# A convolution's last block: its gates moved ahead, twelve of its taps on TensorE, and the order of GpSimd and ScalarE around it

## The chip, the core and the metric

The kernel runs on one core of one Trainium2 chip. The metric is the device time of one execution in microseconds (us); the median of several runs is given. The core has TensorE (matrix products, PE in the profile; PEld is its weight load), VectorE (DVE), ScalarE (ACT), GpSimd (POOL) and SyncE (SP), which issues most transfers. The engines run their own instruction streams and meet through semaphores.

## What is computed

A trunk of two layers over 512 tokens of width 1024, in float32. The first layer mixes tokens by a Conformer convolution, the second by attention; each is followed by a squared-ReLU MLP. Only the convolution matters here:

```python
def conformer_conv(h, pw1_w, pw1_b, dw_w, dw_b, ln_g, ln_b, pw2_w, pw2_b):
    a = h @ pw1_w + pw1_b
    u, gate = jnp.split(a, 2, axis=-1)
    u = u * jax.nn.sigmoid(gate)
    y = depthwise_causal_conv(u, dw_w, width=31) + dw_b
    y = layernorm(y, ln_g, ln_b)
    y = jax.nn.silu(y)
    return y @ pw2_w + pw2_b
```

## The kernel before

Channels lie on the 128 partitions, tokens (512) along the free axis, so the 1024 channels are 8 blocks of 128, numbered j = 0 to 7. A float32 product is made of three matmuls of a high and a low part (hi x hi, lo x hi, hi x lo), and each operand is split into such parts by ScalarE (high) and GpSimd or VectorE (low).

For each block, the first pointwise product gives u and its gate in two PSUM banks. `gates` (VectorE, two instructions) scales both into `tmp`; `sigmoid` (ScalarE) and `gated` (VectorE) put u into `upad`, with 31 columns of padding. The 31 taps of the depthwise convolution are then shared out:

- TensorE takes `PE_TAPS` = 7 of them: a tap is a product with a diagonal matrix, three matmuls for its parts (lines 793 to 795, function `conv`). It needs `uhi` (ScalarE, `u_hi`), `ulo` (GpSimd, `u_lo`) and the block's diagonals `diaghi`, `diaglo`, which ScalarE builds from the identity, 14 small instructions of 128x128 (`diagonals`, line 1205).
- ScalarE makes the first two taps into two PSUM banks (`first_taps`, lines 1274 and 1276; they wait for semaphore `acc`, the join of the block in front) and `POOL_TAPS` = 5 products in SBUF (`pool_taps`, line 1284), which GpSimd adds into `y` in four sums (`tap_sums`, line 500).
- VectorE takes the other 17, one instruction each, in two chains that go on from ScalarE's first two (`tap`, line 1729). `join` adds the two chains into `acc1`, `finish` adds TensorE's bank to it.
- GpSimd's `y_total` adds `acc1` to `y` of that block, and `y` to `sumsq`, the sum over blocks from which the mean is made.

The last block, j = 7, has `MORE_TAPS` = 4 x `LOOP_TAPS` = 8 of VectorE's taps moved to TensorE. Their diagonals (`morehi`, `morelo`) are built ahead by ScalarE, `LOOP_TAPS` taps (4 small instructions) in each of the four blocks of its loop (blocks 2 to 5, `more_diagonals`, line 1197). `conv(KB - 1, 1, MORE_TAPS)` runs these taps first and waits for the block's ordinary diagonals only behind them.

The order on each engine is the order of the code. VectorE runs all 17 taps of block 6 and puts the gates of block 7 behind tap 14 and `gated` behind tap 16 (`last_gates`), then joins block 6, finishes it, and does the 9 taps left of block 7. Once `y` of block 7 is complete on VectorE (line 1807), TensorE sums all blocks into the mean, as a product of `ones` with `sumsq` (line 836) and with `y` of block 7 (line 839), with small products in between whose results nobody reads (`keep_warm`). VectorE subtracts the mean (line 1811), ScalarE squares, TensorE sums the squares by columns, ScalarE takes the root, VectorE the reciprocal, TensorE spreads it, and the normalised blocks go through silu into the second pointwise product (`N_PW2`). Its weights lie in units 0 to 3, split high by ScalarE (`split_hi`) and low by GpSimd (`conv_lo`), units 0 and 1 in block 6 and units 2 and 3 at the end. SyncE refills a pair of units once both low parts are made.

Of the kernel before, what the change touches and what calls it, by code (L numbers as in the profile page):

```python
# [13 lines left out]
KB = D // P  # L14
# [14 lines left out]
LOOP_TAPS = 2  # L29
# [121 lines left out]
def build(nc, x, g_mix_pre, g_mix_post, g_ffn_pre, g_ffn_post, conv_pw1_w, conv_pw1_b, conv_dw_w,  # L151
# [194 lines left out]
    with nc.Block() as block:  # L346
# [105 lines left out]
        def _(pool):  # L452
# [41 lines left out]
            def tap_sums(j):  # L494

                for k in range(1, POOL_TAPS):
                    pool.wait_ge(s["tap_act"], ACT_TAPS * j + (3 + k))
                    if k > 1:
                        pool.wait_ge(s["y_sum"], y_sums(j) + (k - 1))
                    g.tensor_tensor(blk(y, j), blk(y, j), prods[:, k - 1, :], ALU.add).then_inc(s["y_sum"], 1)  # L500
# [7 lines left out]
            def y_total(j, r):  # L508

                at_ = y_sums(j + 1) + POOL_SUMS  # L510
                pool.wait_ge(s["y_done"], j + 1)
                pool.wait_ge(s["y_sum"], at_)
                g.tensor_tensor(blk(y, j), blk(y, j), acc1[:, r, :], ALU.add).then_inc(s["y_sum"], 1)
                pool.wait_ge(s["y_sum"], at_ + 1)
                g.tensor_tensor(sumsq[:, :], sumsq[:, :], blk(y, j), ALU.add).then_inc(s["y_sum"], 1)
# [34 lines left out]
            for u in (0, 1):  # L550
                conv_lo(N_PW2, u)
            tap_sums(KB - 2)
            u_lo(KB - 1, 1)
            y_total(KB - 3, 1)
            tap_sums(KB - 1)
            y_total(KB - 2, 0)
            for u in (2, 3):
                conv_lo(N_PW2, u)
# [49 lines left out]
        def _(pe):  # L608
# [226 lines left out]
            pe.wait_ge(s["y_sum"], y_sums(KB))  # L835
            pe.matmul(psum[:, STAT, :], ones[:, :], sumsq[:, :], start=True, stop=False)
            keep_warm(WARM_TAPS)
# [281 lines left out]
        def _(act):  # L1119
# [159 lines left out]
            def pool_taps(j, r):  # L1279

                for k in range(POOL_TAPS):
# [11 lines left out]
            def conv_step(n, more=None, rs=range(2)):  # L1293
                for r in rs:
# [13 lines left out]
            conv_step(3, None, range(1))  # L1308
            sigmoid(KB - 1)
            u_hi(KB - 1, 1)  # L1310
            first_taps(KB - 1, 1)
            pool_taps(KB - 1, 1)
            for u in (2, 3):
                split_hi(N_PW2, u)
# [324 lines left out]
        def _(dve):  # L1639
# [150 lines left out]
            def last_gates(i):  # L1790

                if i == 14:
                    gates(3, 1)
                if i == 16:
# [19 lines left out]
            d.tensor_tensor(m[:, 7, :], m[:, 6, :], m[:, 7, :], ALU.add).then_inc(s["c_pair"], 1)  # L1814
            inverse(ST_VAR)
# [560 lines left out]
```

## Time and profile before

| | us |
|---|---|
| median of 3 runs | 1178.49 (1177.1 to 1179.14) |
| the profiled execution | 1181.36 |
| its span (first to last instruction) | 1179.7 |
| TensorE busy | 1144.3 (97%) |
| VectorE busy | 907.5 (77%) |
| ScalarE busy | 660.1 (56%) |
| GpSimd busy | 191.1 (16%) |

The profile is of one execution, whose span lies 1.66 us under its own time. The convolution takes the first 178 us or so of it. Matmuls are pipelined: one of 512 columns is shown 0.39 us long, and the next starts 0.23 us after it. "Idle before" in a row is the time the engine stood, with what ended it. The granted clock (PEclk) is 1.00 at 2.4 GHz and 0.50 at 1.2 GHz.

### The profile page before, as it was taken

To read this page: it belongs to the slowest core of one execution; us is meant where nothing else is said; L and a number is where in the kernel's file an instruction comes from. 1 tells how busy PE (TensorE), PEld (TensorE's weight loads), DVE (VectorE), ACT (ScalarE), POOL (GpSimd) and SP (SyncE) were. 2 spreads that over 40 slices of the span, in tenths; PEclk is the share of its full clock that TensorE was granted. 3 is DMA by queue.
4 is the path that set the end of the run, shared out by engine and by line. 5 is a ranking of instruction groups with operands and counts; after the bars stand their busy time and mean duration, and the time that the engine had idled before them with its cause. 6 is when DMAs were issued, how large, how long until landed. Compare 5 with 4: busy or idle time off the path is not lost. (4 is left out here: it accounts for less than half of the span.)

```text
span 1179.7 us, 16069 instructions
## 1 busy us (share of the span) xinstructions
PE 1144.3 (97%) x5598; PEld 962.5 (82%) x5598; DVE 907.5 (77%) x1368; ACT 660.1 (56%) x1106; POOL 191.1 (16%) x176
## 2 busy tenths in 40 slices
PE   7999799999999999999999999999999999999996
PEld 6788688978888888887888888888888888888885
DVE  4899955689479579589888888884797588586698
ACT  4878847566354444345677666665566453443453
POOL 5588860120000000003420001000300000000000
PEclk9999989999999999999999999999999999999998
DMA  4422211520621523412222232222423414215301
GB/s 149 108 71 71 71 39 33 183 69 5 211 73 36 178 72 105 145 36 54 55 54 54 55 87 71 72 72 72 143 72 108 143 36 163 88 36 179 107 19 72
DMA packets 103676, 102.30 MB, mean 87 GB/s; under 512 B 4622, under 2 KB 86542, under 8 KB 103611
## 3 DMA queue, kind: packets, MB, share of 16 engines
q1 hardware_dynamic: 103532, 101.29, 27.0%
q8 instruction: 38, 0.62, 0.2%
q10 hardware_dynamic: 78, 0.16, 0.1%
q14 instruction: 28, 0.22, 0.1%
HBM read 99.34 MB, written 2.10 MB: 86 GB/s over the span
## 5 line engine op out<-in xcount | busy, mean ns | idle before, releaser
L617 PE MATMUL psum<-hhi,whi 128*128 128x512 f32 x792 | 312.6, 395 | 0.6 <-DVE tmp L1908 0.3
L619 PE MATMUL psum<-hhi,wlo 128*128 128x512 f32 x792 | 308.8, 390 | 0.0
L618 PE MATMUL psum<-hlo,whi 128*128 128x512 f32 x792 | 308.5, 390 | 0.0
L1149 ACT ACTIVATE whi<-mraw 128x1024 fp32r<-128x1024 f32 x176 | 185.3, 1054 | 145.1 <-PE psum L884 113.6
L1657 DVE TENSOR_TENSOR wlo<-mraw,whi 128x1024 fp32r<-128x1024 f32 x176 | 213.9, 1221 | 44.4 <-ACT whi L1149 44.4
L882 PE MATMUL psum<-whi,aop_hi 128*128 128x512 f32 x448 | 175.3, 391 | 0.8 <-DVE wlo L1657 0.8
L619 PEld LDWEIGHTS psum<-hhi,wlo 128*128 128x128 f32 x792 | 148.6, 188 | 31.8
L884 PE MATMUL psum<-whi,aop_lo 128*128 128x512 f32 x448 | 174.4, 389 | 0.0
L883 PE MATMUL psum<-wlo,aop_hi 128*128 128x512 f32 x448 | 174.3, 389 | 0.0
L617 PEld LDWEIGHTS psum<-hhi,whi 128*128 128x128 f32 x792 | 148.8, 188 | 30.9 <-issue 2.0
L618 PEld LDWEIGHTS psum<-hlo,whi 128*128 128x128 f32 x792 | 148.8, 188 | 29.1
L1388 ACT ACTIVATE pair<-tmp 128x512 f32<-128x512 f32 x64 | 40.4, 632 | 156.0 <-DVE tmp L1908 156.0
L1908 DVE SCALAR_TENSOR_TENSOR tmp<-psum,rinv 128x512 f32<-128x512 f32 x64 | 44.0, 689 | 78.9 <-PE psum L619 76.3
L882 PEld LDWEIGHTS psum<-whi,aop_hi 128*128 128x128 f32 x448 | 84.1, 188 | 18.2 <-DVE wlo L1657 1.2
L884 PEld LDWEIGHTS psum<-whi,aop_lo 128*128 128x128 f32 x448 | 84.1, 188 | 17.7
L883 PEld LDWEIGHTS psum<-wlo,aop_hi 128*128 128x128 f32 x448 | 84.1, 188 | 17.1
L1729 DVE SCALAR_TENSOR_TENSOR psum<-upad,vec,psum 128x512 f32<-128x512 f32 x120 | 80.5, 752 | 3.6 <-ACT psum L1274 3.6
L1962 DVE TENSOR_TENSOR mraw<-mraw 128x1024 f32<-128x1024 f32 x64 | 78.0, 1221 | 1.7
L1127 ACT ACTIVATE whi<-wraw 128x1024 fp32r<-128x1024 f32 x51 | 52.7, 1050 | 7.8 <-PE psum L619 4.7
L574 POOL CAST wfhi<-wfraw 128x128 fp32r<-128x128 f32 x8 | 5.0, 629 | 302.0 <-DVE wlo L1657 302.0
L624 PE MATMUL psum<-hhi,whi 128*128 128x256 f32 (+1 forms) x128 | 41.6, 325 | 3.5 <-DVE hlo L1663 3.3
L1646 DVE TENSOR_TENSOR wlo<-wraw,whi 128x1024 fp32r<-128x1024 f32 x35 | 42.8, 1225 | 2.6 <-ACT whi L1127 2.6
(253 smaller groups left out, 1946.9 us busy)
## 6 DMA issues: line engine op xcount, KB each, us to landing
mraw<-in_mlp_w_up SPq DMA_DIRECT2D x64, 512.0 KB, 5.3
mraw<-in_mlp_w_down SPq DMA_DIRECT2D x64, 512.0 KB, 4.6
wraw<-in_conv_pw_w SPq DMA_DIRECT2D x20, 512.0 KB, 4.5
wraw<-in_attn_w_in SPq DMA_DIRECT2D x16, 512.0 KB, 4.6
wraw<-in_attn_w_in SPq DMA_DIRECT2D x16, 256.0 KB, 3.1
wraw<-in_attn_w_o SPq DMA_DIRECT2D x8, 512.0 KB, 4.0
xin<-in_x SPq DMA_DIRECT2D x4, 512.0 KB, 6.8
wraw<-in_conv_pw_w SPq DMA_DIRECT2D x8, 256.0 KB, 6.7
```

What stands on the lines that cost most here:

```text
L617: pe.matmul(o, whi[:, u, kb, :], xhi, start=start, stop=False)
L618: pe.matmul(o, whi[:, u, kb, :], xlo, start=False, stop=False)
L619: return pe.matmul(o, wlo[:, u, kb, :], xhi, start=False, stop=stop)
L882: pe.matmul(o, ah, wh, start=kt == 0 and (not kept or c == 0), stop=False)
L883: pe.matmul(o, ah, wl, start=False, stop=False)
L884: return pe.matmul(o, al, wh, start=False, stop=kt == 3 and (not kept or c == CHUNKS - 1))
L1127: a.activation(whi[:, u, :, :], wraw[:, r, :, c * P:(c + 1) * P], ACT.Copy).then_inc(w_hi[r], 2 if single else 1)
L1149: a.activation(split_unit(whi, e), raw_unit(c, e_), ACT.Copy).then_inc(s["m_hi"], 1)
L1657: d.tensor_tensor(split_unit(wlo, e), raw_unit(c, e_), split_unit(whi, e).bitcast(F32), ALU.subtract).then_inc(s["m_ready"], 1)
L1729: d.scalar_tensor_tensor(dst, upad[:, r, t:t + S], vcol(V_DW + t, j), src, ALU.mult, ALU.add).then_inc(s["tap"], 1)
L1908: d.scalar_tensor_tensor(tmp[:, 2 + j % 2, :], psum[:, j % 4, :], 0.0, rinv[:, :], ALU.max, ALU.mult).then_inc(s["up_relu"], 1)
L1962: d.tensor_tensor(to, to, mraw[:, p[PLUS[i]], half], ALU.add).then_inc(s["t_sum"], 1)
```

## The change

- `LOOP_TAPS` is 3, so `MORE_TAPS` is 12: TensorE runs 12 extra taps of block 7, VectorE 5, and ScalarE builds six, not four, extra small diagonals in each of the four looped blocks.
- VectorE does the gates of block 7 behind tap 4 of block 6 and `gated` behind tap 5.
- ScalarE: in block 6 three pool taps come first, then block 7's `sigmoid` and `u_hi`, then the other two; `first_taps` of block 7, its diagonals, its pool taps, and all four splits of `N_PW2` behind.
- GpSimd: in block 6 two sums, `u_lo` of block 7, two sums, then `y_total` of block 5. Behind the sums of block 7 `y_total` of block 6 leaves out the addition into `sumsq`. Only units 0 and 1 of `N_PW2` are split there, behind that total.
- TensorE adds one product of `ones` with `y` of block 6 to the mean. It waits for one count less on `y_sum`.
- VectorE makes the low parts of units 2 and 3 of `N_PW2`, ahead of the reciprocal of the variance.

```diff
-LOOP_TAPS = 2
+LOOP_TAPS = 3
...
-            def y_total(j, r):
+            def y_total(j, r, add=True):
...
                 g.tensor_tensor(blk(y, j), blk(y, j), acc1[:, r, :], ALU.add).then_inc(s["y_sum"], 1)
+                if not add:
+                    return
...
             u_lo(KB - 2, 0)
-            for u in (0, 1):
-                conv_lo(N_PW2, u)
-            tap_sums(KB - 2)
+            tap_sums(KB - 2, range(1, 3))
             u_lo(KB - 1, 1)
+            tap_sums(KB - 2, range(3, POOL_TAPS))
             y_total(KB - 3, 1)
             tap_sums(KB - 1)
-            y_total(KB - 2, 0)
-            for u in (2, 3):
+            y_total(KB - 2, 0, add=False)
+            for u in (0, 1):
                 conv_lo(N_PW2, u)
...
-            pe.wait_ge(s["y_sum"], y_sums(KB))
+            pe.wait_ge(s["y_sum"], y_sums(KB) - 1)
             pe.matmul(psum[:, STAT, :], ones[:, :], sumsq[:, :], start=True, stop=False)
+            pe.matmul(psum[:, STAT, :], ones[:, :], y[:, KB - 2, :], start=False, stop=False)
...
-            conv_step(3, None, range(1))
+            sigmoid(KB - 2)
+            first_taps(KB - 2, 0)
+            u_hi(KB - 2, 0)
+            pool_taps(KB - 2, 0, range(3))
             sigmoid(KB - 1)
             u_hi(KB - 1, 1)
+            pool_taps(KB - 2, 0, range(3, POOL_TAPS))
             first_taps(KB - 1, 1)
+            next_diagonals(KB - 2, 0)
             pool_taps(KB - 1, 1)
-            for u in (2, 3):
+            for u in range(4):
                 split_hi(N_PW2, u)
...
-                if i == 14:
+                if i == 4:
                     gates(3, 1)
-                if i == 16:
+                if i == 5:
                     gated(KB - 1, 1)
...
             d.tensor_tensor(m[:, 7, :], m[:, 6, :], m[:, 7, :], ALU.add).then_inc(s["c_pair"], 1)
+            for u in (2, 3):
+                split_lo(N_PW2, u)
             inverse(ST_VAR)
```

On ScalarE, from the splits in block 6 to the products of block 7. Before (of the 14 diagonals the first two stand):

```order
L1127 ACTIVATE whi<-wraw 128x1024 [waits unit0,raw0] x2
L1284 ACTIVATE y<-upad,vec 128x512
L1284 ACTIVATE prods<-upad,vec 128x512 [waits y_sum] x4
L1205 ACTIVATE diaghi<-ident,dwhi 128x128 [waits conv_done]
L1205 ACTIVATE diaglo<-ident,dwlo 128x128
L1259 ACTIVATE tmp<-tmp,vec 128x512 [waits glu_g]
L1266 ACTIVATE uhi<-upad 128x544 [waits conv_done,glu_u]
L1274 ACTIVATE psum<-upad,vec 128x512 [waits acc,glu_u]
L1276 ACTIVATE psum<-upad,vec 128x512
L1284 ACTIVATE y<-upad,vec 128x512
L1284 ACTIVATE prods<-upad,vec 128x512 [waits y_sum] x4
```

In the changed kernel, from the `uhi` of block 6, with the first two diagonals:

```order
L1268 ACTIVATE uhi<-upad 128x544 [waits conv_done,glu_u]
L1286 ACTIVATE y<-upad,vec 128x512
L1286 ACTIVATE prods<-upad,vec 128x512 [waits y_sum] x2
L1261 ACTIVATE tmp<-tmp,vec 128x512 [waits glu_g]
L1268 ACTIVATE uhi<-upad 128x544 [waits conv_done,glu_u]
L1286 ACTIVATE prods<-upad,vec 128x512 [waits y_sum] x2
L1276 ACTIVATE psum<-upad,vec 128x512 [waits acc,glu_u]
L1278 ACTIVATE psum<-upad,vec 128x512
L1207 ACTIVATE diaghi<-ident,dwhi 128x128 [waits conv_done]
L1207 ACTIVATE diaglo<-ident,dwlo 128x128
L1286 ACTIVATE y<-upad,vec 128x512
L1286 ACTIVATE prods<-upad,vec 128x512 [waits y_sum] x4
```

The sigmoid and `uhi` of block 7 have moved up into block 6's products, and the diagonals from ahead of that sigmoid to behind the two instructions that wait for `acc`.

On GpSimd, from `ulo` of block 6 to the end of the taps. Before:

```order
L491 TENSOR_TENSOR ulo<-upad,uhi 128x544 [waits u_hi]
L505 TENSOR_TENSOR wlo<-wraw,whi 128x1024 [waits w_hi0] x2
L500 TENSOR_TENSOR y<-y,prods 128x512 [waits tap_act]
L500 TENSOR_TENSOR y<-y,prods 128x512 [waits y_sum,tap_act] x3
L491 TENSOR_TENSOR ulo<-upad,uhi 128x544 [waits u_hi]
L513 TENSOR_TENSOR y<-y,acc_73 128x512 [waits y_sum,y_done]
L515 TENSOR_TENSOR sumsq<-sumsq,y 128x512 [waits y_sum]
L500 TENSOR_TENSOR y<-y,prods 128x512 [waits tap_act]
L500 TENSOR_TENSOR y<-y,prods 128x512 [waits y_sum,tap_act] x3
L513 TENSOR_TENSOR y<-y,acc_73 128x512 [waits y_sum,y_done]
L515 TENSOR_TENSOR sumsq<-sumsq,y 128x512 [waits y_sum]
```

In the changed kernel:

```order
L491 TENSOR_TENSOR ulo<-upad,uhi 128x544 [waits u_hi]
L500 TENSOR_TENSOR y<-y,prods 128x512 [waits tap_act]
L500 TENSOR_TENSOR y<-y,prods 128x512 [waits y_sum,tap_act]
L491 TENSOR_TENSOR ulo<-upad,uhi 128x544 [waits u_hi]
L500 TENSOR_TENSOR y<-y,prods 128x512 [waits y_sum,tap_act] x2
L513 TENSOR_TENSOR y<-y,acc_73 128x512 [waits y_sum,y_done]
L517 TENSOR_TENSOR sumsq<-sumsq,y 128x512 [waits y_sum]
L500 TENSOR_TENSOR y<-y,prods 128x512 [waits tap_act]
L500 TENSOR_TENSOR y<-y,prods 128x512 [waits y_sum,tap_act] x3
L513 TENSOR_TENSOR y<-y,acc_73 128x512 [waits y_sum,y_done]
```

The two splits into `wlo` ahead of block 6's sums are gone; `ulo` of block 7 stands between these sums; the last addition into `sumsq` is gone.

On VectorE, from the taps of block 6 to its join. Before:

```order
L1729 SCALAR_TENSOR_TENSOR psum<-upad,vec,psum 128x512 [waits tap_act] x2
L1729 SCALAR_TENSOR_TENSOR psum<-upad,vec,psum 128x512 [waits tap] x13
L1740 TENSOR_TENSOR tmp<-psum,rinv 128x512 [waits glu_u,unit1]
L1742 TENSOR_TENSOR tmp<-psum,rinv 128x512
L1729 SCALAR_TENSOR_TENSOR acc_73<-upad,vec,psum 128x512 [waits y_sum,tap]
L1729 SCALAR_TENSOR_TENSOR psum<-upad,vec,psum 128x512 [waits tap]
L1754 SCALAR_TENSOR_TENSOR upad<-tmp,vec 128x512 [waits u_ready,tap_act,glu_s,glu_t]
L1760 TENSOR_TENSOR acc_73<-psum,acc_73 128x512 [waits tap]
```

In the changed kernel:

```order
L1736 SCALAR_TENSOR_TENSOR psum<-upad,vec,psum 128x512 [waits tap_act] x2
L1736 SCALAR_TENSOR_TENSOR psum<-upad,vec,psum 128x512 [waits tap] x3
L1747 TENSOR_TENSOR tmp<-psum,rinv 128x512 [waits glu_u,unit1]
L1749 TENSOR_TENSOR tmp<-psum,rinv 128x512
L1736 SCALAR_TENSOR_TENSOR psum<-upad,vec,psum 128x512 [waits tap]
L1761 SCALAR_TENSOR_TENSOR upad<-tmp,vec 128x512 [waits u_ready,tap_act,glu_s,glu_t]
L1736 SCALAR_TENSOR_TENSOR psum<-upad,vec,psum 128x512 [waits tap] x9
L1736 SCALAR_TENSOR_TENSOR acc_73<-upad,vec,psum 128x512 [waits y_sum,tap]
L1736 SCALAR_TENSOR_TENSOR psum<-upad,vec,psum 128x512 [waits tap]
L1767 TENSOR_TENSOR acc_73<-psum,acc_73 128x512 [waits tap]
```

The two gates and the writing of `upad` for block 7 have moved up by ten and eleven taps.

## Rows read from the trace of the kernel before

**Rows 1.** Window: busy us (instructions) PE, PEld, DVE, ACT, POOL; PEclk, DMA share, GB/s.

```profile
104.00:120.00 16.00, 16.00 (x72) 13.14 (x71) 15.49 (x23) 13.04 (x31) 14.26 (x10) 1.00 0.20 66
```

**Rows 2.** Timeline of VectorE, blocks 6 and 7: start, us, operation, [idle before].

```profile
130.07 1.78 DVE L1754 SCALAR_TENSOR_TENSOR upad<-tmp,vec 128x512 f32<-128x512 f32 x1
...
132.71 9.97 DVE L1729 SCALAR_TENSOR_TENSOR psum<-upad,vec,psum 128x512 f32<-128x512 f32 x15 [0.26 <-ACT psum L1274]
142.59 0.69 DVE L1740 TENSOR_TENSOR tmp<-psum,rinv 128x512 f32<-128x512 f32 x1
...
145.10 0.98 DVE L1754 SCALAR_TENSOR_TENSOR upad<-tmp,vec 128x512 f32<-128x512 f32 x1
146.00 0.68 DVE L1760 TENSOR_TENSOR acc<-psum,acc 128x512 f32<-128x512 f32 x1
...
156.44 0.69 DVE L1804 TENSOR_TENSOR acc<-acc,y 128x512 f32<-128x512 f32 x1 [2.10 <-POOL y L500]
160.61 0.69 DVE L1807 TENSOR_TENSOR y<-psum,acc 128x512 f32<-128x512 f32 x1 [3.48 <-PE psum L795]
163.15 4.88 DVE L1811 SCALAR_TENSOR_TENSOR y<-psum,y 128x512 f32<-128x512 f32 x8 [1.85 <-PE psum L839]
...
172.05 0.18 DVE L1679 RECIPROCAL irms<-rms 128x4 f32<-128x4 f32 x1 [2.49 <-ACT rms L1180]
```

**Rows 3.** Timeline of TensorE, blocks 6 and 7 and the statistics.

```profile
136.16 0.39 PE L793 MATMUL psum<-uhi,diaghi 128*128 128x512 f32 x1
...
148.24 0.80 PE L793 MATMUL psum<-uhi,morehi 128*128 128x512 f32 x1 [7.02 <-POOL ulo L491]
...
155.44 0.39 PE L793 MATMUL psum<-uhi,diaghi 128*128 128x512 f32 x1
...
160.34 1.02 PE L836 MATMUL psum<-sumsq,ones 128*128 128x512 f32 x2
161.20 1.05 PE L635 MATMUL psum<-ones 128*128 128x128 f32 x8
```

**Rows 4.** Timeline of ScalarE, blocks 6 and 7.

```profile
129.00 0.72 ACT L1259 ACTIVATE tmp<-tmp,vec 128x512 f32<-128x512 f32 x1 [0.63 <-DVE tmp L1740]
...
138.74 0.39 ACT L1205 ACTIVATE diaghi<-ident,dwhi 128x128 fp32r<-128x128 f32 x1
...
142.54 0.39 ACT L1205 ACTIVATE diaglo<-ident,dwlo 128x128 fp32r<-128x128 f32 x1
...
146.78 0.78 ACT L1274 ACTIVATE psum<-upad,vec 128x512 f32<-128x512 f32 x1
...
148.11 0.71 ACT L1284 ACTIVATE y<-upad,vec 128x512 f32<-128x512 f32 x1
148.72 2.55 ACT L1284 ACTIVATE prods<-upad,vec 128x512 f32<-128x512 f32 x4
```

**Rows 5.** Timeline of GpSimd, blocks 5 to 7.

```profile
130.02 1.29 POOL L513 TENSOR_TENSOR y<-y,acc 128x512 f32<-128x512 f32 x1
...
133.94 1.37 POOL L491 TENSOR_TENSOR ulo<-upad,uhi 128x544 fp32r<-128x544 f32 x1 [0.94 <-ACT uhi L1266]
...
150.74 5.60 POOL L500 TENSOR_TENSOR y<-y,prods 128x512 f32<-128x512 f32 x4
156.47 1.80 POOL L513 TENSOR_TENSOR y<-y,acc 128x512 f32<-128x512 f32 x1
```

**Rows 6.** Page, part 5: a split of 128x1024 on VectorE.

```profile
L1657 DVE TENSOR_TENSOR wlo<-mraw,whi 128x1024 fp32r<-128x1024 f32 x176 | 213.9, 1221 | 44.4 <-ACT whi L1149 44.4
```

**Rows 7.** Timeline of TensorE in a later stage.

```profile
584.67 0.39 PE L975 MATMUL psum<-hhi,wfhi 128*128 128x256 f32 x1 [1.51 <-DVE hlo L2131]
```

**Rows 8.** Windows of that stage, TensorE: busy us (instructions), PEclk, DMA share, GB/s.

```profile
585.00:585.50 0.50, 0.50 (x5) 0.55 0.00 0
...
591.50:592.00 0.50, 0.50 (x5) 0.62 0.00 0
```

**Rows 9.** Window of rows 1's kind, in the convolution's norm.

```profile
172.00:173.00 1.00, 1.00 (x7) 1.00 (x6) 0.18 (x1) 0.98 (x2) 0.00 (x0) 0.52 0.00 0
```

More of the change, by code:

```diff
@@ L492, in u_lo, with tap_sums @@
                                 ALU.subtract).then_inc(s["u_ready"], 1)
-            def tap_sums(j):
-                for k in range(1, POOL_TAPS):
+            def tap_sums(j, ks=range(1, POOL_TAPS)):
+                for k in ks:
                     pool.wait_ge(s["tap_act"], ACT_TAPS * j + (3 + k))
@@ L1277, in first_taps, with pool_taps @@
                              scale=vcol(V_DW + 1, j)).then_inc(s["tap_act"], 1)
-            def pool_taps(j, r):
-                for k in range(POOL_TAPS):
+            def pool_taps(j, r, ks=range(POOL_TAPS)):
+                for k in ks:
                     if k > 0 and not (isinstance(j, int) and j == 0):
@@ L1291, in next_diagonals, with conv_step @@
                 diagonals(j + 1, 1 - r)
-            def conv_step(n, more=None, rs=range(2)):
-                for r in rs:
+            def conv_step(n, more=None):
+                for r in range(2):
                     j = 2 * n + r
```

## The prediction

> **What bounds the kernel now.** I read the stage table first: in a block of the convolution's loop TensorE is busy for all 16.00 us and VectorE for 15.49 [rows 1], so neither ScalarE's nor GpSimd's work there sets the time, as long as it fits. Then the timelines of the four engines around the last two blocks (6 and 7), because the diff changes nothing else of weight. The reader is to see who is last there. VectorE finishes its taps, stands 2.10 us for GpSimd's sums and 3.48 us for TensorE, and writes y[7] at 160.61 [rows 2]. TensorE had stood 7.02 us before block 7's taps, because VectorE's gates for block 7 come behind 15 taps of block 6, and it ran the first of those taps at half rate [rows 3]. GpSimd ended its sums for block 7 at 156.34 and its total of block 6 at 158.27; the addition into sumsq behind it, of the length of the total at 130.02 (1.29), brings it to about 159.6 [rows 5], just ahead of TensorE's need at 160.34 [rows 3]. So before, TensorE is last and GpSimd is 0.7 us behind being last. Everything after hangs on the mean: VectorE's subtraction starts at 163.15 [rows 2], and all later stages follow that point one for one, since TensorE, VectorE and ScalarE work in a chain from there to the second pointwise product. I therefore work out where 163.15 goes.
>
> **The sum is made against the profiled execution** (1181.36 us, span 1179.7); the median of the three runs is 1178.49, 2.87 lower. I carry the difference over to the median unchanged.
>
> **Loop.** Each of the four looped blocks gets 2 more small diagonals on ScalarE, 2 x 0.292 us = 0.58 ([rows 4]: 13 steps of them from 138.74 to 142.54). ScalarE stands 0.63 us ahead of the sigmoid that follows [rows 4], so 0.05 is left, and VectorE waits for nothing else of ScalarE there. Cost 0; if the cover were gone it would be under 0.1 a block. The splits of the convolution weights grow by 4 columns of 8 blocks at the start: nothing that I can price above 0.05.
>
> **Gates of block 7 earlier.** Block 6's taps start at 132.71 and take 9.97 for 15, 0.665 each [rows 2]; five end at 136.0. The gates also wait for TensorE's last unit, whose last matmul lies right ahead of the first tap matmul of block 6 at 136.16 [rows 3] and so ends at about 136.3; with 0.1 us of signalling the gates start at 136.45. Before, 2.51 us lay from gates to gated (142.59 to 145.10) with two taps between [rows 2]; now there is one, so gated starts at 138.3. From gated's start to TensorE's first tap matmul it took 3.14 us (145.10 to 148.24 [rows 2, 3]), so TensorE starts block 7 at 141.45. It has just ended block 6 (21 matmuls from 136.16 at 0.233, [rows 3]: 21 from 155.44 to 160.34). The pause of 7.02 shrinks to about 0.3, and the slow start goes: before, 24 matmuls took 7.20 us against 24 x 0.233 = 5.6. That is the gain, 6.8 + 1.6 us of TensorE.
>
> **Twelve taps on TensorE.** 12 x 3 = 36 matmuls x 0.233 = 8.4: they end at 149.85. VectorE keeps 5 taps of block 7, not 9 (2.7 us less).
>
> **Where it goes wrong: the diagonals.** The seven ordinary taps of block 7 need their diagonals. Before, ScalarE built them at 138.74, ahead of block 7's sigmoid. Now they stand behind first_taps of block 7, and these wait for `acc`, the join of block 6, which VectorE reaches only behind the remaining 11 taps. gated ends and the next operation starts 0.90 later (145.10 to 146.00 [rows 2]), at 139.2; 11 x 0.665 = 7.3 gives the join at 146.5. Before, first_taps came 0.78 behind the join's start (146.00 to 146.78 [rows 2, 4]): now 147.3, against 146.78. ScalarE, which has only uhi (from gated's end) and two products of 0.61 to do, stands from about 141.2 till then. first_taps take 1.33 (146.78 to 148.11), so the diagonals run from 148.6, 14 x 0.292 = 4.1, to 152.7. TensorE stands from 150.0 to 152.9, then runs 21 x 0.233 = 4.9 to 157.9 if its clock holds.
>
> **GpSimd's sums become last.** ScalarE's products for GpSimd (the pool taps) of block 7 come behind the diagonals: the first at 152.7, the second ends 0.61 + 0.71 later, 154.05 [rows 4]. GpSimd's four sums start at 154.15; from their start to the total behind them is 5.73 (150.74 to 156.47 [rows 5]), so the total of block 6 starts at 159.9, 3.4 us later than before. It takes 1.80 where VectorE adds y and acc1 from 0.03 us ahead of it (156.44 [rows 2]), and 1.29 where it is itself 0.05 ahead (130.02, and VectorE's instruction at 130.07 then takes 1.78 [rows 2, 5]). The last sum of block 7 releases the same two again, so I take 1.80: 161.7, lower bound 161.2. The sum into sumsq is no longer waited for (GpSimd does not do it). VectorE's y[7] is written by about 161.3 and is not last.
>
> The Trainium skill (SBUF — State Buffer, section "SBUF: two separate sides") says that VectorE operations with two SBUF inputs and GpSimd operations exclude each other for a whole instruction, whichever starts first. By that rule the total is 1.80 if VectorE starts first again; both pairs of rows agree, and without the rule the sum would be 0.5 lower.
>
> **The extra matmul.** From TensorE's first statistic matmul to VectorE's subtraction it was 160.34 to 163.15 = 2.81 us. The new one on y[6] is the same form, two passes, 0.86 (160.34 to 161.20 [rows 3]). 161.75 + 2.81 + 0.86 = 165.4: **+2.3 us** against 163.15, with the clock at its upper level (2.4 GHz).
>
> **The clock.** TensorE now pauses 2.9 us (150.0 to 152.9) and 3.8 us (157.9 to 161.7), with only 4.9 us of work between. In this trace a pause of 1.51 us before 584.67 was followed by a granted clock of 0.55 in the half us from 585.0, that is, mostly the lower level of 1.2 GHz, which lasted until about 591.6; and the 7.02 us pause by the 1.6 us of loss above [rows 3, 7, 8]. The statistic matmuls (3.5 us of work) would run partly slow. Bounds: 0 and 1.6 us. Since the pause is longer than the one at 584.67, I take 1.1. Of the stretch behind it I take no change: before, the clock was already low from 172.0 [rows 9].
>
> **Two splits on VectorE.** The low parts of two weight units leave GpSimd and stand between the pair sum and the reciprocal. VectorE stands 2.49 us there [rows 2]; 2 x 1.221 = 2.44 [rows 6]. Cost 0 to 0.1. On SP's queue the refill of these units waits for these splits, and the small loads stand behind it; what they bring is used only in the second half of the second pointwise product and later: nothing. On GpSimd the other two splits come behind the total, two of them where two stood before, ahead of the squares that GpSimd adds, which move by the sum themselves. Nothing.
>
> Sum: +2.3 + 1.1 = +3.4. 1181.36 + 3.4 = 1184.8 for the profiled execution, **1178.5 + 3.4 = 1181.9 for the median**.
>
> **Rivals.** 0.2% is 2.4 us, about what a measurement of this kernel can tell from no change.
> (a) *The order costs little*: the total takes 1.29, the clock holds, and with the pauses elsewhere the half-rate stretch at 172 (granted clock 0.52 [rows 9]; it delays the broadcast, by my estimate some 0.9 us) falls away: +1.8 - 0.9 = +0.9, or +1.8 without the last: 1179.4 to 1180.3, no change. For it: a clock's fall is not seen behind every short pause. Chance 0.26.
> (b) *gated meets GpSimd.* gated took 1.78 at 130.07 while GpSimd's total ran (130.02), 0.98 at 145.10 [rows 2, 5]. GpSimd's two sums of block 6 now start behind its ulo, at 135.3 [rows 5], and end at 135.3 + 2 x 1.40 (5.60 for four) = 138.1, 0.2 ahead of gated. If they are 0.2 late, gated, the 11 taps, the join, the diagonals and the sums all come 0.8 later: +4.2, 1182.7. Chance 0.12; it decides from a sum that ends behind 138.3.
> (c) *Faster, by the clock alone.* A later stage ran at half rate from 585.0 to 591.5 [rows 8], which costs 6.5 / 2 = 3.2 us, and the stretch at 172 costs 0.9. Both hang on where pauses fall. If the shift moved the pauses so that both stayed at 2.4 GHz, and the statistics too: +1.8 - 0.9 - 3.2 = -2.3, and -2.6 if the signals come 0.3 sooner than taken: 1175.9. It decides if the granted clock in the stage behind 582 stays at 1.00. Against it: the median of the runs lies 2.87 below the profiled one, so these may not have that stretch to lose. Chance 0.07.
> (d) *The change does what it is named for* and the diagonals are not waited for: TensorE ends at 141.45 + 57 x 0.233 = 154.7, and the pool taps come right behind first_taps, at 148.6. Their second product ends at 149.9, the sums lead to the total at 150.0 + 5.73 = 155.7, it ends at 157.5, and the subtraction starts at 157.55 + 3.67 = 161.2: -1.9, 1176.6. That needs ScalarE to build the diagonals in its pause before the join, and the order of its instructions in the program says that it doesn't. Chance 0.02.
>
> **How the numbers follow.** The forecast has 0.53, (a) 0.26, (b) 0.12, (c) 0.07, (d) 0.02. Slower: forecast 0.53 + (b) 0.12 = 0.65, less 0.01 at the edge; same 0.28 with (a) and (d); faster 0.08. Range: from (a)'s middle with its clock gain, 1178.8, to (b) with the full 1.6 of clock (+2.3 + 0.8 + 1.6 = +4.7) and 1 us for later stages, 1184.2.
>
> **What would show it.** In the changed kernel: TensorE's taps of block 7 start near 141.5 with nearly no pause; 36 matmuls; then a pause of 2.9 ended by ScalarE's diagonals; first_taps of block 7 near 147.3, idle ScalarE for some 6 us before; GpSimd's first sum of block 7 near 154.2 and the total to 161.7; the first statistic matmul released by GpSimd, and VectorE's subtraction between 165.4 and 167. Wrong if the subtraction comes before 163.2, or if TensorE ends the taps after GpSimd's total.

## The result

The changed kernel ran at a median of 1184.45 us (1182.08 to 1185.74, 6 runs) against 1177.62 us (1176.76 to 1179.14, 6 runs), and the ratio of the times is 1.0044, 95% interval 1.0031 to 1.0057. It is slower. (The ratio is the one on record for the whole comparison; the two medians alone lie 6.83 us or 0.58% apart, a little outside the interval.) The same kernel, measured once more beside the kernel before in a later comparison (e9_again below), came out at 1.0016 (1.0006 to 1.0027). So the loss is there both times, and its size is not one number; what of it the runs explain is said below.

Head of the page of the profiled execution (its own time 1184.01 us): span, TensorE's busy time, and the granted clock in 40 slices.

```profile
span 1182.3 us, 16112 instructions
...
PE 1147.0 (97%) x5612; PEld 962.7 (81%) x5612; DVE 907.1 (77%) x1366; ACT 662.7 (56%) x1114; POOL 185.4 (16%) x173
...
PEclk9999999999999999999999999999999999999998
```

The timelines of the changed kernel, in which rows 2 to 5 have their counterparts. VectorE first: start, length, operation, idle before.

```profile
136.44 0.69 DVE L1747 TENSOR_TENSOR tmp<-psum,rinv 128x512 f32<-128x512 f32 x1 [0.26 <-PE psum L620]
...
138.31 0.75 DVE L1761 SCALAR_TENSOR_TENSOR upad<-tmp,vec 128x512 f32<-128x512 f32 x1
...
146.34 0.69 DVE L1767 TENSOR_TENSOR acc<-psum,acc 128x512 f32<-128x512 f32 x1
...
159.61 0.69 DVE L1811 TENSOR_TENSOR acc<-acc,y 128x512 f32<-128x512 f32 x1 [7.56 <-POOL y L500]
160.34 0.69 DVE L1814 TENSOR_TENSOR y<-psum,acc 128x512 f32<-128x512 f32 x1
166.95 4.88 DVE L1818 SCALAR_TENSOR_TENSOR y<-psum,y 128x512 f32<-128x512 f32 x8 [5.92 <-PE psum L841]
...
173.27 2.35 DVE L1653 TENSOR_TENSOR wlo<-wraw,whi 128x1024 fp32r<-128x1024 f32 x2
175.93 0.18 DVE L1686 RECIPROCAL irms<-rms 128x4 f32<-128x4 f32 x1 [0.31 <-ACT rms L1182]
```

Gates at 136.44 and gated at 138.31 are where 142.59 and 145.10 were [rows 2]. From there to the join of block 6 at 146.34 nothing waits. Behind its taps of block 7 VectorE stands 7.56 us for GpSimd, writes y of block 7 at 160.34, 0.27 earlier than before, and stands 5.92 us for TensorE: the subtraction starts at 166.95, against 163.15 [rows 2]. The two splits (2.35) fit in front of the reciprocal.

ScalarE and GpSimd:

```profile
139.65 1.32 ACT L1286 ACTIVATE prods<-upad,vec 128x512 f32<-128x512 f32 x2
147.13 0.78 ACT L1276 ACTIVATE psum<-upad,vec 128x512 f32<-128x512 f32 x1 [6.15 <-DVE acc L1767]
...
148.47 0.39 ACT L1207 ACTIVATE diaghi<-ident,dwhi 128x128 fp32r<-128x128 f32 x1
...
152.56 0.71 ACT L1286 ACTIVATE y<-upad,vec 128x512 f32<-128x512 f32 x1
```

```profile
153.96 5.56 POOL L500 TENSOR_TENSOR y<-y,prods 128x512 f32<-128x512 f32 x4 [7.28 <-ACT prods L1286]
159.66 1.77 POOL L513 TENSOR_TENSOR y<-y,acc 128x512 f32<-128x512 f32 x1
```

`first_taps` of block 7 come at 147.13 behind the join, with 6.15 us of idle time before them; before, they came at 146.78 [rows 4]. Behind them stand the 14 diagonals (148.47 to 152.5) and only then the products, at 152.56 instead of 148.11. GpSimd waits 7.28 us for the second product, starts its sums at 153.96 instead of 150.74 and the total at 159.66 instead of 156.47 [rows 5].

TensorE, and its granted clock in three windows of half a microsecond (third number from the end):

```profile
141.24 0.51 PE L794 MATMUL psum<-uhi,morehi 128*128 128x512 f32 x1
...
152.70 0.50 PE L794 MATMUL psum<-uhi,diaghi 128*128 128x512 f32 x1 [2.79 <-ACT diaglo L1207]
...
161.48 1.95 PE L837 MATMUL psum<-sumsq,ones 128*128 128x512 f32 x2 [3.63 <-POOL y L513]
163.22 1.92 PE L838 MATMUL psum<-y,ones 128*128 128x512 f32 x2
...
165.89 1.02 PE L841 MATMUL psum<-y,ones 128*128 128x512 f32 x2
```

```profile
162.00:162.50 0.50, 0.50 (x2) 0.50 0.00 0
...
165.00:165.50 0.50, 0.50 (x6) 0.94 0.00 0
...
592.50:593.00 0.50, 0.50 (x4) 0.50 0.00 0
```

It starts block 7 at 141.24, 7.0 us earlier than before, stands 2.79 us for the diagonals and 3.63 us for GpSimd's total, and runs the two first statistic products at 1.2 GHz: 1.95 and 1.92 us, against 1.02 [rows 3].

### The profile page after: what moved, and what is told of

Its sections match the earlier page's. It is cut to its first block and busy times, and to the rows that moved or that the text cites. A ratio compares the mean times of both kernels' runs of the same rounds, so it can differ in the third digit from the quotient of the medians.

```text
span 1182.3 us, 16112 instructions
## 1 busy us (share of the span) xinstructions
PE 1147.0 (97%) x5612; PEld 962.7 (81%) x5612; DVE 907.1 (77%) x1366; ACT 662.7 (56%) x1114; POOL 185.4 (16%) x173
## 5 line engine op out<-in xcount | busy, mean ns | idle before, releaser
L884 PE MATMUL psum<-whi,aop_hi 128*128 128x512 f32 x448 | 175.3, 391 | 0.8 <-DVE wlo L1664 0.8
L1736 DVE SCALAR_TENSOR_TENSOR psum<-upad,vec,psum 128x512 f32<-128x512 f32 x116 | 78.1, 752 | 3.6 <-ACT psum L1276 3.6
```

What stands on the lines that cost most here:

```text
L884: pe.matmul(o, ah, wh, start=kt == 0 and (not kept or c == 0), stop=False)
L1736: d.scalar_tensor_tensor(dst, upad[:, r, t:t + S], vcol(V_DW + t, j), src, ALU.mult, ALU.add).then_inc(s["tap"], 1)
```

## The experiments

The same point of the program lies up to a microsecond apart in the profiles (`gated` of block 6 starts between 129.38 and 130.45), so points are counted from that start (130.07 before, 130.16 in the changed kernel), where all these kernels are still alike. The fourth column is a length, the others are starts; all are in us.

| kernel | first_taps of block 7 | total of block 6 | first statistic product | from it to the subtraction | subtraction | ratio of the times (95%) |
|---|---|---|---|---|---|---|
| before | 16.71 | 26.40 | 30.27 | 2.81 | 33.08 | 1 |
| changed | 16.97 | 29.50 | 31.32 | 5.47 | 36.79 | 1.0044 (1.0031 to 1.0057) |
| e9_again | 16.99 | 29.53 | 31.36 | 3.77 | 35.13 | 1.0016 (1.0006 to 1.0027) |
| e1_diag_first | 17.00 | 25.49 | 27.32 | 5.45 | 32.77 | 0.9992 (0.9980 to 1.0003) |
| e2_warm | 16.98 | 29.53 | 34.23 | 3.67 | 37.90 | 1.0040 (1.0025 to 1.0055) |
| e10_warm16 | 16.98 | 29.52 | 31.35 | 3.78 | 35.13 | 1.0014 (1.0002 to 1.0027) |
| e3_eight_taps | 17.03 | 29.54 | 31.37 | 3.77 | 35.14 | 1.0004 (0.9991 to 1.0017) |
| e4_full_total | 16.96 | 29.50 | 32.67 | 2.92 | 35.59 | 1.0021 (1.0011 to 1.0031) |
| e5_before_twelve | 16.71 | 26.38 | 34.34 | 2.81 | 37.15 | 1.0026 (1.0015 to 1.0036) |
| e6_splits_back | 17.01 | 29.54 | 31.37 | 5.47 | 36.84 | 1.0039 (1.0022 to 1.0057) |
| e7_free | 10.71 | 22.26 | 24.47 | 3.66 | 28.13 | 0.9940 (0.9918 to 0.9961) |
| e12_free_again | 10.72 | 22.24 | 24.50 | 3.67 | 28.17 | 0.9959 (0.9945 to 0.9972) |
| e8_nowait_only | 10.71 | 23.30 | 25.14 | 3.78 | 28.92 | 0.9960 (0.9945 to 0.9975) |
| e11_free_eight | 10.73 | 22.17 | 25.92 | 3.67 | 29.59 | 0.9959 (0.9946 to 0.9973) |

**Is the chain through ScalarE the cause?** e1_diag_first moves one call of the changed kernel:

```diff
+            next_diagonals(KB - 2, 0)
             first_taps(KB - 1, 1)
-            next_diagonals(KB - 2, 0)
             pool_taps(KB - 1, 1)
```

> The changed kernel with one step moved: ScalarE builds block 7's diagonals ahead of first_taps of block 7, in its pause of 6.15 us before the join. The theory (the end of the stage is set by the chain join, first_taps, diagonals, pool taps, GpSimd's four sums, total): the products start at 148.5 instead of 152.56, the total ends 4.1 us earlier, at 157.3, TensorE has no pause between its 12 and its 7 taps and ends at 154.5, and VectorE's subtraction comes at 161.1 to 162.9 instead of 166.95: 4.1 to 5.9 us faster than the changed kernel, 0.3 to 2.1 faster than the kernel before. Rival (the extra matmuls and the pause of TensorE set the time, not GpSimd's sums): the subtraction moves by less than 2 us.

Timeline of that kernel, TensorE's first statistic product and VectorE's subtraction:

```profile
157.15 1.54 PE L837 MATMUL psum<-sumsq,ones 128*128 128x512 f32 x2 [2.63 <-POOL y L513]
...
162.60 4.87 DVE L1818 SCALAR_TENSOR_TENSOR y<-psum,y 128x512 f32<-128x512 f32 x8 [5.90 <-PE psum L841]
```

The total came 4.01 us earlier (29.50 to 25.49), as theory had it, and with it the subtraction (36.79 to 32.77). The statistics ran at 1.2 GHz again (5.45 from their start to the subtraction), so it came at the slow end of what was expected. The time falls back to that of the kernel before. TensorE has no pause before its ordinary taps here and still stands 2.63 us for GpSimd's total, so it is not TensorE's matmuls or its pause that cost the 4 us, but the 14 diagonals in front of GpSimd's products.

**And if ScalarE need not wait?** e7_free takes away the reason for the wait (block 7's first taps write banks 0 and 1, the chains that the join of block 6 ends lie in banks 6 and 7) and puts the products ahead of the diagonals:

```diff
-                if not (isinstance(j, int) and j == 0):
+                if not (isinstance(j, int) and j in (0, KB - 1)):
                     act.wait_ge(s["acc"], j)
...
             first_taps(KB - 1, 1)
-            next_diagonals(KB - 2, 0)
             pool_taps(KB - 1, 1)
+            next_diagonals(KB - 2, 0)
```

> The changed kernel, where first_taps of block 7 no longer wait for the join of block 6 (they write banks 0 and 1, which that join does not read), and the order behind them on ScalarE is pool taps, then diagonals. Theory: first_taps at 140.9, the five products end at about 144.7, diagonals at 148.7, before TensorE asks for them at 149.9; GpSimd's sums of block 7 run 146.7 to 152.3 and the total to 154.2; TensorE runs 57 matmuls without a pause to 154.5 and goes on into the statistics; the subtraction at 158.2. That is 8.7 us earlier than the changed kernel and 5.0 earlier than the kernel before: 1172.6 against a median of 1177.6. Rival (the two-SBUF-input meetings of VectorE and GpSimd and the clock eat it): 160 or later.

Timeline of e7_free over all engines, the rows that moved:

```profile
141.14 0.77 ACT L1276 ACTIVATE psum<-upad,vec 128x512 f32<-128x512 f32 x1
...
146.92 5.62 POOL L500 TENSOR_TENSOR y<-y,prods 128x512 f32<-128x512 f32 x4
...
154.90 1.02 PE L837 MATMUL psum<-sumsq,ones 128*128 128x512 f32 x2
...
158.56 4.87 DVE L1818 SCALAR_TENSOR_TENSOR y<-psum,y 128x512 f32<-128x512 f32 x8 [2.71 <-PE psum L841]
```

ScalarE goes on at 141.14 without a pause, GpSimd's sums follow its sumsq at 146.92, and TensorE comes from its last tap straight to the statistics at 154.90. The subtraction lies 28.13 behind gated, 4.95 us less than before (expected 5.0). The median was 1172.03 beside 1178.94 before (0.9940). e12_free_again is the same kernel on another chip.

> e7_free once more, for more executions: 0.994 to 0.996 of the kernel before, subtraction 28.1 behind gated of block 6. If the first result was a matter of the clock in a few executions, the ratio comes out nearer to 0.998.

28.17 and 0.9959 (1173.23 beside 1178.95): the place is the same to 0.04 us, and this version beats both kernels, each time.

e8_nowait_only takes only the wait away and keeps the order.

> The changed kernel, where only the wait of first_taps of block 7 for the join of block 6 is gone; the order on ScalarE stays first_taps, diagonals, pool taps. Counted from the start of gated of block 6 (130.16 in the changed kernel, whose subtraction comes 36.8 behind it; 33.1 in the kernel before; 28.1 in e7_free): first_taps at +10.8, diagonals to +16.2, the second product ends at +17.6, the sums at +23.3, the total at +25.1, subtraction at +28.8. So the wait is worth nearly all, and the order diagonals before products costs 0.7 against e7_free. Rival (the order matters as much as the wait): +31 or more.

ScalarE's `first_taps` and VectorE's subtraction in e8_nowait_only:

```profile
140.12 0.77 ACT L1276 ACTIVATE psum<-upad,vec 128x512 f32<-128x512 f32 x1
...
158.33 4.87 DVE L1818 SCALAR_TENSOR_TENSOR y<-psum,y 128x512 f32<-128x512 f32 x8 [3.48 <-PE psum L841]
```

The subtraction lies at 28.92, with a ratio of 0.9960: the wait is worth 6.2 us of the chain (against 35.13 in e9_again, statistics at 2.4 GHz in both), the order behind it 0.8.

**The twelve taps.** e3_eight_taps is the changed kernel with `LOOP_TAPS = 2`.

> The changed kernel with 8 instead of 12 extra taps of block 7 on TensorE, all else as changed. Theory: TensorE's 12 fewer matmuls end 2.8 us earlier, at 146.8, and only lengthen its pause before the diagonals (still at 152.65); VectorE's four more taps end at 154, ahead of GpSimd's sums at 159.5. The subtraction stays at 166.9 within 0.2, unless the longer pause lowers the clock earlier. Rival (TensorE's 36 matmuls for extra taps cost time): 2.8 us faster.

TensorE in e3_eight_taps:

```profile
151.99 0.79 PE L794 MATMUL psum<-uhi,diaghi 128*128 128x512 f32 x1 [5.58 <-ACT diaglo L1207]
...
160.77 1.12 PE L837 MATMUL psum<-sumsq,ones 128*128 128x512 f32 x2 [1.40 <-POOL y L513]
```

The statistics start at 31.37 against 31.32: in the order of the work the four taps more on TensorE move nothing. The subtraction is 1.65 earlier than in the changed kernel, though, because the clock fell at 150.1, in the longer pause of 5.58 us, and was back at 2.4 GHz at 156.9, before the statistics. In that profile this is the clock and not the taps: e9_again shows the same 3.77 with twelve. In the executions the two can't be told apart. Of e3_eight_taps ten lie between 1179.1 and 1182.4 us, eight of them within 0.7 us of each other; of the twelve-tap kernel twelve lie between 1179.2 and 1183.1 in e9_again and six between 1182.1 and 1185.7 in the first comparison. That the longer pause puts the fall of the clock under the taps every time, and that twelve taps cost time in this way, was not tested.

e5_before_twelve does the twelve taps alone, in the kernel before (`LOOP_TAPS = 3` there and nothing else).

> The kernel before with 12 instead of 8 extra taps of block 7 on TensorE and nothing else. Before, TensorE was the last to end the taps, so 12 more matmuls at 0.233 us put all behind it off by 2.8 us: subtraction at 165.9 to 166.0 against 163.15. Rival (VectorE's four taps fewer help): no later than before.

Its timeline, TensorE's first tap and first statistic product and VectorE's subtraction:

```profile
147.90 0.80 PE L793 MATMUL psum<-uhi,morehi 128*128 128x512 f32 x1 [7.01 <-POOL ulo L491]
...
164.08 1.02 PE L836 MATMUL psum<-sumsq,ones 128*128 128x512 f32 x2
...
166.89 4.88 DVE L1811 SCALAR_TENSOR_TENSOR y<-psum,y 128x512 f32<-128x512 f32 x8 [1.85 <-PE psum L839]
```

+4.07 where 2.8 was expected: 12 matmuls at 0.233 are 2.8. For the other 1.3 the clock accounts: it stayed at 1.2 GHz for 6.1 us from the first tap at 147.90 (3.2 us before), and half of the difference is 1.45 us. Where TensorE is last, as in the kernel before, the taps cost; and the ratio of 1.0026 (3.1 us) says the same.

e11_free_eight is e7_free with eight.

> e7_free with 8 instead of 12 extra taps of block 7 on TensorE. Theory: with ScalarE free, GpSimd's total ends at +24.1 behind gated of block 6 and TensorE's 57 matmuls at +24.5, so the two are level; with 45 matmuls TensorE ends at +21.7 and waits for GpSimd; VectorE's nine taps end its y[7] at about +25.8, ahead of the product that needs it (+26.8). Subtraction at +27.8, 0.3 earlier than e7_free, or the same: the twelve taps bring nothing there. Rival (the twelve taps pay once ScalarE is out of the way): 1 us or more later.

Timeline of e11_free_eight, TensorE and VectorE:

```profile
149.16 0.50 PE L794 MATMUL psum<-uhi,diaghi 128*128 128x512 f32 x1 [2.39 <-ACT diaglo L1207]
...
154.09 2.06 DVE L1811 TENSOR_TENSOR acc<-acc,y 128x512 f32<-128x512 f32 x1
...
155.72 1.02 PE L837 MATMUL psum<-sumsq,ones 128*128 128x512 f32 x2
```

1.46 later than e7_free, not 0.3 earlier. Two things were left out. The first are the diagonals: with the products ahead of them they are ready at 149.1, so TensorE, done with eight taps at about 146.8, stands 2.39 us for them; with twelve it comes to them when they are ready. The 2.8 us of taps taken off thus made only a pause: 21 matmuls at 0.233 behind 149.16 end 24.3 behind `gated`, where e7_free has its statistics at 24.47. The second is the clock, which was at 1.2 GHz from 150.6 to 154.0, under these 21 matmuls; half of that, 1.7 us, is by my estimate what put the statistics at 25.92. VectorE, with four more taps, also met GpSimd's split in its addition (2.06 us instead of 0.69). The time is nevertheless that of e7_free on the same chip (0.9959 both), so between 8 and 12 taps nothing is decided by time.

**The clock.** e2_warm and e10_warm16 fill TensorE's pause before the statistics with small products whose results nobody reads, 30 of them in e2_warm (shown), 16 in e10_warm16:

```diff
+            keep_warm(30, 2)
             pe.wait_ge(s["y_sum"], y_sums(KB) - 1)
```

> The changed kernel with 30 small matmuls of TensorE, whose results nobody reads, in its pause of 3.63 us between block 7's last tap and the first statistic matmul, so that it doesn't stand. Clock theory: the granted clock stays at 1.00 there, the time from the first statistic matmul (161.48) to the subtraction shrinks from 5.47 to 3.67, and the subtraction comes at 165.1 to 165.3: 1.7 to 1.8 us faster than the changed kernel, if the later stages don't change. Rival (the new product on y[6] waits for memory or for something else, the clock is not the cause): 5.47 stays.

> The changed kernel with 16 small matmuls of TensorE in its pause before the first statistic matmul; 30 of them took 6.3 us, 2.8 more than the pause holds, so 16 take 3.4 and end with it. Clock theory: the first statistic matmul stays at 161.5, the stretch from it to VectorE's subtraction is 3.67 and not 5.47, the subtraction comes at 165.2, 1.8 earlier than in the changed kernel, and the granted clock stays at 1.00 from 140 to the norm. Rival: the pause of 3.0 us before the diagonals is enough to lower the clock, and it doesn't help.

TensorE in e2_warm, then in e10_warm16:

```profile
164.34 1.02 PE L838 MATMUL psum<-sumsq,ones 128*128 128x512 f32 x2
```

```profile
161.46 1.12 PE L838 MATMUL psum<-sumsq,ones 128*128 128x512 f32 x2
```

In e2_warm the 30 products ran past the pause: the statistics started 2.9 us late (34.23), but took 3.67 and not 5.47, and the granted clock stayed at 1.00 through the whole stage. I had made the filling too long: the subtraction came 1.1 later than in the changed kernel, and the time stayed that of the changed kernel (1.0040). With 16 the statistics started on time, 31.35, and took 3.78. So the clock costs 1.7 us of the statistics in the changed kernel's profile. The executions don't show this gain: 1.0014 against 1.0016 of e9_again, which has no filling. In the profile of e9_again the fall came earlier:

> The changed kernel itself, once more, for more executions beside the kernel before. In the profiles VectorE's subtraction comes 3.8 us later than before; if that is all, like executions (with the same mean granted clock) differ by 3.8 to 4.3 us, and the ratio is 1.003 to 1.004; if the change costs more in executions without a profile, it is 1.005 or more.

Timeline of e9_again, TensorE:

```profile
151.94 0.50 PE L794 MATMUL psum<-uhi,diaghi 128*128 128x512 f32 x1 [2.77 <-ACT diaglo L1207]
...
160.74 1.13 PE L837 MATMUL psum<-sumsq,ones 128*128 128x512 f32 x2 [2.08 <-POOL y L513]
```

Windows of e9_again:

```profile
153.50:154.00 0.50, 0.50 (x3) 0.50 0.00 0
...
161.00:161.50 0.50, 0.50 (x2) 1.00 0.00 0
```

The clock fell at 153.3 and rose at 156.7, under the tap matmuls, where GpSimd's sums cover it; at 161 it is 1.00 and the statistics take 3.77. So the same program has two courses, and the nine profiles with the extra product and without filling fall into the same two: 3.66 to 3.78 from the first statistic product to the subtraction, or 5.45 to 5.47. In e9_again the norm was faster, too: from the reciprocal to the first normalised block (VectorE's first product with the spread root) it is 1.82 us, where it was 3.34 before and 3.37 in the changed kernel. These are VectorE's rows in the kernel before, the changed kernel and e9_again:

```profile
175.39 1.28 DVE L1819 TENSOR_TENSOR y<-y,psum 128x512 f32<-128x512 f32 x2 [3.17 <-PE psum L668]
```

```profile
179.30 1.29 DVE L1828 TENSOR_TENSOR y<-y,psum 128x512 f32<-128x512 f32 x2 [3.19 <-PE psum L669]
```

```profile
173.41 0.18 DVE L1686 RECIPROCAL irms<-rms 128x4 f32<-128x4 f32 x1 [0.22 <-ACT rms L1182]
175.23 1.29 DVE L1828 TENSOR_TENSOR y<-y,psum 128x512 f32<-128x512 f32 x2 [1.64 <-PE psum L669]
```

TensorE at the same place, first in the kernel before, then in e9_again: ten products whose results nobody reads, queued ahead of the spreading of the root, and the spreading (L668, L669).

```profile
171.57 2.08 PE L635 MATMUL psum<-ones 128*128 128x128 f32 x10
173.44 1.91 PE L668 MATMUL psum<-ident,irms 128*128 128x128 f32 x8
```

```profile
172.94 1.36 PE L636 MATMUL psum<-ones 128*128 128x128 f32 x10
174.13 1.06 PE L669 MATMUL psum<-ident,irms 128*128 128x128 f32 x8
```

At the lower clock both are slow, and the spreading has to wait behind the slow filling too: it starts 1.39 us behind the reciprocal in the kernel before and 0.72 in e9_again. That is one reason why the spans can lie the other way (1177.9 in e9_again, 1179.7 before), though the subtraction comes 2.05 us later in e9_again, with its statistics at 2.4 GHz in both: the norm gave back 1.5 of it, and the stage around 590 (below) the rest.

**The extra product and the splits.** e4_full_total undoes the shortening of GpSimd's last total:

```diff
-            y_total(KB - 2, 0, add=False)
+            y_total(KB - 2, 0)
...
-            pe.wait_ge(s["y_sum"], y_sums(KB) - 1)
+            pe.wait_ge(s["y_sum"], y_sums(KB))
             pe.matmul(psum[:, STAT, :], ones[:, :], sumsq[:, :], start=True, stop=False)
-            pe.matmul(psum[:, STAT, :], ones[:, :], y[:, KB - 2, :], start=False, stop=False)
```

> The changed kernel with the addition of y of block 6 into sumsq back on GpSimd and without TensorE's extra product of ones with y of block 6. GpSimd needs 1.3 us more before TensorE starts the statistics (162.8 instead of 161.5), and TensorE 0.86 less at 2.4 GHz or 1.7 less at 1.2 GHz. Theory: subtraction between 166.5 and 167.4, within 0.5 of the changed kernel's 166.95, so this edit is worth little either way. Rival (the extra matmul is what makes the change slow): 1 us or more faster.

35.59, with the statistics at 2.4 GHz: 1.31 later at their start, 0.85 shorter, 0.46 later than e9_again. So this edit of the change is a gain of about half a microsecond; against the changed kernel's 36.79 the clock hides it.

e6_splits_back puts all four splits back on GpSimd.

> The changed kernel with all four low parts of the second product's first weights on GpSimd, none on VectorE. Theory: VectorE's reciprocal starts as the root ends, 8.90 behind the subtraction's start, as in the other kernels; GpSimd's additions of the squares start up to 0.5 later and are not waited for: no change of any point of the chain (under 0.1 us). Rival (VectorE's two splits of 2.35 us delay the reciprocal, or GpSimd's late additions delay the root): 0.3 us or more either way.

GpSimd and VectorE in e6_splits_back, by time:

```profile
170.63 1.28 POOL L562 TENSOR_TENSOR sumsq<-m 128x512 f32<-128x512 f32 x1
...
172.52 1.28 DVE L1821 TENSOR_TENSOR m<-m 128x512 f32<-128x512 f32 x1 [0.70 <-ACT m L1326]
176.51 0.18 DVE L1686 RECIPROCAL irms<-rms 128x4 f32<-128x4 f32 x1 [2.71 <-ACT rms L1182]
```

This expectation fell. GpSimd's additions of the squares start at 170.63 instead of 170.18, and VectorE's pair sum, which reads two SBUF operands, took 1.28 instead of 0.83 beside them; the reciprocal came 9.56 behind the subtraction where all others have 8.9 to 9.0. The two splits on VectorE cost at most 0.1 us there and save 0.6 against this profile. Half of that is the late pair sum: TensorE's last sums of the squares start 0.3 later. The other half is the clock, which fell at 175.3 in both profiles, here with more of these sums still to run (1.41 us against 1.11). (The ratio, 1.0039, does not tell it from the changed kernel.)

## Why the prediction was right, and where its numbers were off

The direction and the chain behind it came as forecast: the subtraction was put at 166.5 (163.15 + 3.4) and came at 166.95. The size in whole executions is less sure. By the ratio of 1.0044 the forecast median of 1178.49 becomes 1183.7, inside the range of 1178.8 to 1184.2; the measured median, 1184.45, lies 0.25 above the range, and the two medians are twice the forecast +3.4 apart. The terms one by one:

- **The loop costs nothing**: right. `gated` of block 6 lies at 130.16 against 130.07, and ScalarE's sigmoid at 129.09 waits for nothing, its reserve just used up.
- **Gates**: 136.45, 138.3 and TensorE at 141.45 were forecast; 136.44, 138.31 and 141.24 came. gated did not meet GpSimd (0.75), so rival (b) is out.
- **The diagonals and first_taps**: join 146.5, first_taps 147.3, products 152.7, pause of TensorE 2.9 forecast; 146.34, 147.13, 152.56 and 2.79 came. e1, e7 and e8 show that this chain is the cause and not only beside it.
- **GpSimd last**: total 159.9 to 161.7 forecast, 159.66 to 161.43 came (1.77, with VectorE's addition 0.05 ahead). First statistic product 161.75 forecast, 161.48 came.
- **The extra product**: 0.86 at 2.4 GHz. Right where the clock was up (e10: 3.78 from the first statistic product to the subtraction, forecast 3.67).
- **The clock** is the term that was mis-sized. I took 1.1 between bounds of 0 and 1.6; it was 1.7 in the profile of the changed kernel and 0.1 in e9_again. In these profiles it is never a value between, but one or the other, by whether the fall lands on the taps or on the statistics.
- **Later stages unchanged**: wrong in kind. For the kernel before, 1016.55 us lie from the subtraction to the end, for the changed kernel 1015.35, for e9_again 1013.39. The rows above show 1.5 of e9_again's difference in the norm. The rest is the stage around 590, where the granted clock was low for 6.8 us in the kernel before (585.05 to 591.88, not to 591.5 as the prediction reads [rows 8]) and for 3.4 us in the changed kernel (a window of it stands above) and in e9_again. With the stretch from the subtraction to the first normalised block taken off, the profiles sort by this alone: 1000.9 to 1002.1 us where the clock stayed up there (e2, e4, e5, e8, e10, e11), 1002.5 to 1003.0 with 3.4 us of low clock (changed, e9, e3, e12), 1003.6 to 1005.2 with 6.8 (before, e1, e6, e7).
- **The difference carried over from the profiled execution to the median**: wrong. The profiled execution of the kernel before was a long one (1181.36, 2.87 above its median, with 6.8 us of low clock around 590), that of the changed kernel was not (1184.01, 0.44 below its median). From profile to profile the change costs 2.65 us, from median to median 6.83.
- **The lower end of the range**, 1178.8, does not follow from rival (a)'s own numbers, 1179.4 to 1180.3.

The forecast of +3.4 lay between the two measurements: 0.44% is 5.2 us, 0.16% is 1.9. That it lay between is in part luck, since two of its terms, the clock as a mean and the later stages as nothing, were wrong. The runs explain 2.05 us by the order of work (e9_again, e10_warm16 and e3_eight_taps agree within 0.01) and 1.7 by the clock in the statistics. Executions fall into groups by their mean granted clock: in the first comparison the changed kernel took 1182.1 to 1184.0 at 0.993 to 0.995 and 1184.9 to 1185.7 at 0.990, in e9_again all twelve took 1179.2 to 1183.1 at 0.993 to 0.994; in the later comparisons the kernel before took 1176.9 to 1179.6 at 0.991 to 0.993 and 1180.8 to 1182.0 at 0.989 to 0.990. Three of the six executions of the changed kernel in the first comparison were at 0.990 and none of the twelve in e9_again, which is likely a part of the difference between the two. Why the first comparison gave 0.44% and the second 0.16%, with intervals that do not touch, stays open beyond that. Kernels with the changed kernel's chain came out at 1.0014 to 1.0021 on the chip of e9_again, and at 1.0040, 1.0004 (e2_warm, e3_eight_taps) and 1.0039 (e6_splits_back) on two others, which does not sort by chip (e2_warm's subtraction came 1.1 later, e6_splits_back's reciprocal 0.6), and I ran nothing that fixes the place of the clock's fall in executions without a profile.

Rival (a) is what e9_again comes near to: statistics at 2.4 GHz and no low stretch in the norm, which gave back 1.5 us where (a) had 0.9; only its total took 1.77 and not 1.29. Rival (c), faster by the clock alone, was no more than half seen: the clock did move 1.5 us in the norm, and the six kernels whose clock stayed up around 590 took 2.3 to 3.4 us less than the kernel before outside the norm (forecast 3.2); no median of the changed kernel fell below that of before, though. Rival (d) was the right mechanism to name. e1_diag_first is its order, and its subtraction came at 32.77 behind `gated` where (d) has 31.0 (161.2 less 130.16), the 1.8 between them being the lower clock in the statistics; e7_free, which drops the wait too, had a median of 1172.0.

## What to carry to other kernels

When work is moved ahead on one engine, list for each of the others what it still has in front of the next thing that somebody waits for: here TensorE got its input 7 us earlier and GpSimd its own 3.2 us later, since one wait on ScalarE, stricter than the buffers need, held 14 small instructions and the products behind them. A wait kept for all iterations of a loop can be needless in the last one, written out behind the loop, where the buffers differ; taking it away was worth 6.2 us of the chain, and turned a loss into a gain. When a profile is the base of a sum for the median, look first at where its own execution lies among the others. Where a pause lets TensorE's clock fall, ask which work runs slow behind it: under another engine's longer work it costs nothing; where nothing else covers the products, here in the statistics, it costs up to their length again.

## What the runs showed of the hardware

- The clock's fall is not fixed to a program. Two profiles of the same kernel had it from 161.7 to 165.0 and from 153.3 to 156.7, with the same two pauses of 2.8 us and then 3.6 us or, after slower taps, 2.1. A fall cost the statistics 1.7 us, and the filling and the spreading of the root 1.5 us. Around 590 TensorE pauses 1.51 us in the kernel before, the changed kernel and e2_warm alike, and was then at the lower clock for 6.8 us, for 3.4 us and not at all.
- In these traces a TensorE without a pause was no sure sign that the clock holds: in the kernel before and in the changed kernel it fell at 172.0 and at 175.3 while the timeline shows TensorE running small products without a pause, and in e9_again it did not.
- The Trainium skill describes (TensorE: Matmul & The Clock Gate, section "HAM oscillation — how this bites in real kernels") a kernel in which a wait for a transfer sends TensorE back to the lower clock, so that the next products start cold, and it advises to arrange the work so that TensorE stays warm. The traces here agree in part: in e9_again the clock was still at 1.00 when TensorE came back from its pause of 2.77 us at 151.94, and fell at 153.3. Filling the second pause, as e10_warm16 does, took the price out of the statistics (5.47 to 3.78), though its ratio (1.0014) is that of e9_again (1.0016); where the fall lands under the taps anyway, as in e9_again's profile, there is nothing to win in the statistics.
- VectorE and GpSimd slowed each other where both ran operations with two SBUF inputs: VectorE's addition took 2.06 us instead of 0.69 (e11_free_eight, beside a split) and its pair sum 1.28 instead of 0.83 (e6_splits_back), and GpSimd's total took 1.77 where VectorE's addition had started 0.05 ahead (changed kernel), 1.29 where it had not (e11_free_eight).
